# Modulation products spread over the projection and attention preparation, no barriers between layers, DeltaNet blocks read by a gather

## The reference

```python
def modulation(cond, w_mod, b_mod):
    m = jnp.einsum('...d,de->...e', jax.nn.silu(cond), w_mod) + b_mod
    return split_cols(m, (D_MODEL, D_MODEL, D_MODEL))
...
for l in range(DEPTH):
    shift, scale, gate = modulation(c, w_mod[l], b_mod[l])
    h = rms_norm(xs, norm_w[l]) * (1.0 + scale[:, None, :]) + shift[:, None, :]
    out, _ = mixer(h, lp, (cache_k[:, l], cache_v[:, l], state_gdn[:, l], state_ssm[:, l]))
    xs = xs + gate[:, None, :] * out
y_sample = rms_norm(xs, final_norm_w)
```

## Time and profile before

| | us |
|---|---|
| median of 3 runs | 4798.93 (4793.77 to 4803.2) |
| the profiled execution's own time | 4772.26 |
| its span | 4770.5 |
| PE, PEld busy | 4117.2 (86%), 3850.1 (81%) |
| DVE, ACT, POOL busy | 2153.1 (45%), 1038.3 (22%), 600.1 (13%) |
| mean DMA rate | 104 GB/s |

### The profile page before, as it was taken

The page is one execution under the profiler, slowest core; times in us unless marked ns, Lnnn a source line. Parts: engine busy times, 40 slices in busy tenths (PEclk is TensorE's granted clock), DMA queues, the critical chain, the costliest instruction groups (busy, mean ns, idle before and its releaser), DMA issues.

```text
span 4770.5 us, 64010 instructions
## 1 busy us (share of the span) xinstructions
PE 4117.2 (86%) x24849; PEld 3850.1 (81%) x24849; DVE 2153.1 (45%) x2548; ACT 1038.3 (22%) x1855; POOL 600.1 (13%) x725
## 2 busy tenths in 40 slices
PE   6999999974898968868879999999649989678698
PEld 2999999974887838868849999999648877478688
DVE  3432541116665782245345235311266667723563
ACT  2110111013444510220021012010233454102200
POOL 0010000025100150000000000000350002400000
PEclk7999999987998979989989999999859989789799
DMA  6222222225002442533252222222530034435332
GB/s 225 83 90 81 80 89 94 84 93 192 13 14 77 158 159 95 159 120 115 78 182 91 87 79 85 89 93 75 172 102 14 14 100 158 141 109 164 102 123 92
DMA packets 421562, 497.62 MB, mean 104 GB/s; under 512 B 77602, under 2 KB 357508, under 8 KB 413772
## 3 DMA queue, kind: packets, MB, share of 16 engines
q1 hardware_dynamic: 354840, 384.79, 24.5%
q0 software_dynamic: 33856, 94.70, 5.3%
q10 hardware_dynamic: 32636, 15.04, 1.1%
HBM read 325.08 MB, written 169.37 MB: 104 GB/s over the span
## 4 chain that ended last, share of the span: by engine, by line
PE 71%; DVE 7%; DMA 6%; issue 6%; SPq 3%; DVEq 3%; POOL 2%; ACT 1%; POOLq 1%; ACTq 1%
PE PSUM L680 15%; PE PSUM L682 14%; PE PSUM L681 14%; PE PSUM L1121 5%; PE PSUM L1268 4%; PE PSUM L1142 3%; PE PSUM L1110 2%; PE PSUM L1111 2%; SPq L899 2%; PE PSUM L1371 1%; PE PSUM L1372 1%; PE PSUM L1373 1%; DMA g_XY<-xy_d 1%; PE PSUM L1227 1%; DMA xin<-proj_d 1%
## 5 line engine op out<-in xcount | busy, mean ns | idle before, releaser
L680 PE MATMUL PSUM<-h_hi,w_hi 128*128 128x384 f32 x3456 | 1160.3, 336 | 38.2 <-DVEq L526 30.0
L681 PE MATMUL PSUM<-h_lo,w_hi 128*128 128x384 f32 x3456 | 1158.6, 335 | 0.0
L682 PE MATMUL PSUM<-h_hi,w_lo 128*128 128x384 f32 x3456 | 1158.2, 335 | 0.0
L680 PEld LDWEIGHTS PSUM<-h_hi,w_hi 128*128 128x128 f32 x3456 | 652.1, 189 | 39.3 <-issue 30.2
L681 PEld LDWEIGHTS PSUM<-h_lo,w_hi 128*128 128x128 f32 x3456 | 652.2, 189 | 0.0
L682 PEld LDWEIGHTS PSUM<-h_hi,w_lo 128*128 128x128 f32 x3456 | 651.9, 189 | 0.0
L664 DVE CAST w_hi<-w_raw 128x2048 fp32r<-128x2048 f32 (+1 forms) x104 | 118.9, 1143 | 722.6 <-PE PSUM L682 584.1
...
L680 PE MATMUL PSUM<-b_hi,w_hi 128*128 128x384 f32 x768 | 263.7, 343 | 27.9 <-DVE w_lo L666 10.8
L1121 PE MATMUL PSUM<-v_all,prob_t 128*128 128x64 f32 x2336 | 283.6, 276 | 2.3 <-DVE prob_t L2260 2.2
L1121 PEld LDWEIGHTS PSUM<-v_all,prob_t 128*128 128x128 f32 x2336 | 279.1, 196 | 4.6 <-issue 3.5
L681 PE MATMUL PSUM<-b_lo,w_hi 128*128 128x384 f32 x768 | 261.9, 341 | 0.0
...
## 6 DMA issues: line engine op xcount, KB each, us to landing
...
```

The costliest lines, as they stand in the source:

```text
L680: pe.matmul(dst, wh, x_hi[:, k, lo:hi], start=(k == 0), stop=False)
L681: pe.matmul(dst, wh, x_lo[:, k, lo:hi], start=False, stop=False)
L682: last = pe.matmul(dst, wl, x_hi[:, k, lo:hi], start=False, stop=(k == kt - 1))
```

## The change

- *Norm without a stage of its own.* The squares of x are made block by block as the output projection finishes them, and the sums directly after the last; barriers 0 and 13 and the first one are gone. The final norm takes its factors from the same sums.
- *Modulation by rows.* At the start four pieces of 512 columns (shift and scale) have a buffer each. The gate's four pieces of 256 columns are multiplied after each of the first four runs of the projection (`gate_products`), and shift and scale of the next layer in eight pieces of 256 columns, one behind each tile of attention preparation (`next_load`, `next_columns`). The last layer does that too, on the same weights.
- *First group by k.* The projection's first group is multiplied block by block as h is made (`first_group`), with both accumulators in use at once; DVE splits its weights before it makes h.
- *Loads at the start*: four x buffers instead of two, and the small vector loads issued by POOL ahead of everything, for the second layer during the output projection.
- *DeltaNet preparation*: the block stores of SP and POOL are gone, POOL issues each row load as soon as its buffer is filled, and other fills come later.
- *Blocks by gather*: in attention preparation SP reads the blocks out of `gdn_tile_d` into `u_raw`, in 40 transfers of rows of 128 bytes (`blocks_in`).

```diff
-        def blocks_out(e, t, d):
-            for c in range(4):
-                at = slice(c * SOLVE, (c + 1) * SOLVE)
-                src = g_out[t % 2][at, 6 * d].rearrange("p (h t) -> p h t", t=P)[:, :, at]
-                dst = adiag_d[d, c * 32 + t * 4:c * 32 + t * 4 + 4] if t < NS else adiag_p_d[d].rearrange("(h c) n -> c h n", c=4)[c]
-                e.dma_start(dst.rearrange("h (j i) -> j h i", i=SOLVE), src).then_inc((g_pstored if d else g_stored)[t % 2], 16)
+        def blocks_in(e, c, d):
+            at = slice(c * SOLVE, (c + 1) * SOLVE)
+            for h in range(GH):
+                e.dma_start(u_raw[c * 32 + h:c * 32 + 32:GH, d].rearrange("t (j i) -> t j i", i=SOLVE),
+                            gdn_tile_d[0:NS, at, 6 * d, h * P + c * SOLVE:h * P + c * SOLVE + SOLVE]).then_inc(beta_in, 16)
+            e.dma_start(u_raw[32 * d + c:32 * d + 16:4, 2].rearrange("h (j i) -> h j i", i=SOLVE),
+                        gdn_tile_d[NS, at, 6 * d].rearrange("j (h t) -> h j t", t=P)[:, :, at]).then_inc(beta_in, 16)
...
-                if t >= 2:
-                    sp.wait_ge(tok_turned, t - 1)
+                if t >= 4:
+                    sp.wait_ge(tok_turned, t - 3)
                 src = xsm[t * P:(t + 1) * P] if t < NS else A["x_prompt"].rearrange("b t d -> (b t) d")
-                sp.dma_start(x_tok[t % 2][:], src).then_inc(tok_in[t % 2], 16)
-            sp.drain().then_inc(phase_done, 1)
+                sp.dma_start(x_in[t % 4][:], src).then_inc(x_loaded[t % 4], 16)
+            wm = A["w_mod"][0].rearrange("(k p) n -> p k n", p=P)
+            for g in range(4):
+                sp.dma_start(w_mod[g][:], wm[:, :, g * 2 * GW:(g + 1) * 2 * GW]).then_inc(mod_in[g], 16)
+            sp.dma_start(rope[:], rope_table.rearrange("p (t a d) -> p t a d", t=NT, a=2)).then_inc(cst_in, 16)
+            sp.wait_ge(mod_used, 1)
...
+                def gate_load(r):
+                    if r == 0:
+                        for b in range(2):
+                            sp.wait_ge(x_out[b], l * 64 + 64)
+                            sp.sem_inc(waits_held, 1)
+                        sp.wait_ge(h_made, l * KT + KT)
+                    else:
+                        sp.wait_ge(mod_used, gate_done(l, r - 1))
+                    at = 2 * D_MODEL + r * GW
+                    sp.dma_start(w_gate[:], A["w_mod"][l].rearrange("(k p) n -> p k n", p=P)[:, :, at:at + GW]).then_inc(mod_in[2], 16)
...
+                    if run < 4:
+                        gate_load(run)
...
-                    sp.wait_ge(g_stored[p], (l + 1) * (5 - p) * 5 * 16)
-                    sp.wait_ge(g_pstored[p], (l + 1) * (5 - p) * 4 * 16)
-                for d in range(2):
-                    sp.dma_start(u_raw[:, d], adiag_d[d]).then_inc(beta_in, 16)
-                    sp.dma_start(u_raw[32 * d:32 * d + 16, 2], adiag_p_d[d]).then_inc(beta_in, 16)
...
+                    sp.wait_ge(g_stored[p], (l + 1) * (5 - p) * 16)
+                def next_load(g):
+                    if g >= 2:
+                        sp.wait_ge(mod_used, next_done(l, g - 2))
+                    src = A["w_mod"][NEXT].rearrange("(k p) n -> p k n", p=P)
+                    sp.dma_start(w_next[g % 2][:], src[:, :, g * GW:(g + 1) * GW]).then_inc(mod_in[g % 2], 16)
+                next_load(0)
+                next_load(1)
+                for t in range(2, 10):
+                    if t < NT:
+                        sp.wait_ge(transposed, nth(l, t - 1, 1, 5))
+                        ain_load(t, t % 2)
+                    if t >= 4:
+                        next_load(t - 2)
+                    blocks_in(sp, (t - 2) // 2, t % 2)
...
+            def norm_sums(i):
+                pe.wait_ge(n_add, i * (KT - 1) + KT - 1)
+                for t in range(NT):
+                    last = pe.matmul(bank(6, 1, t), tmp[:, t * P:(t + 1) * P], ones[:, 0:1], start=True, stop=True)
+                last.then_inc(n_mm, 1)
+            def mod_product(dst, w):
+                for k in range(KT):
+                    last = pe.matmul(dst, cond[:, k:16:8], w[:, k], start=(k == 0), stop=(k == KT - 1))
+                last.then_inc(mod_used, 1)
...
+            pe.wait_ge(cond_t, 3)
+            for g in range(4):
+                pe.wait_ge(mod_in[g], 16)
+                if g >= 2:
+                    pe.wait_ge(mod_row, g - 1)
+                mod_product(bank(4 + g % 2)[0:2], w_mod[g])
+                if g == 1:
+                    norm_sums(0)
+            pe.wait_ge(mod_row, 4)
+            mod_columns(mod_rows, 16, 7, 0).then_inc(mod_used, 1)
...
+                def first_group():
+                    pe.wait_ge(w_ready[0], split_count(l, 0) + 2)
+                    pe.wait_ge(acc_free[0], l * NG + 1)
                     for k in range(KT):
...
+                        pe.wait_ge(h_made, l * KT + k + 1)
+                        for b in range(2):
+                            wh = w_hi[0][:, k, b * P:b * P + P]
+                            wl = w_lo[0][:, k, b * P:b * P + P]
+                            for c in range(3):
+                                lo, hi = c * THIRD, (c + 1) * THIRD
+                                dst = bank(3 * b + c, THIRD)
+                                pe.matmul(dst, wh, h_hi[:, k, lo:hi], start=(k == 0), stop=False)
+                                pe.matmul(dst, wh, h_lo[:, k, lo:hi], start=False, stop=False)
+                                last = pe.matmul(dst, wl, h_hi[:, k, lo:hi], start=False, stop=(k == KT - 1))
+                            if k == KT - 1:
+                                last.then_inc(acc_ready[b], 1)
+                def gate_products(run):
+                    if run < 4:
+                        if run:
+                            pe.wait_ge(mod_row, rows_done(l, run - 1))
+                        pe.wait_ge(mod_in[2], 16 + (l * 4 + run + 1) * 16)
+                        mod_product(bank(6, GW)[0:2], w_gate)
+                    elif run == 4:
+                        pe.wait_ge(mod_row, rows_done(l, 3))
+                        pe.sem_inc(waits_held, 1)
+                        mod_columns(gate_rows, 8, 7, 0).then_inc(mod_used, 1)
...
+                    begun = 0
+                    if run == 0:
+                        begun = 2
+                        first_group()
+                        multiply_group(pe, l, 1, 1, 0, KT, h_hi, h_lo)
+                    groups(pe, base + begun, 2 * pairs - begun, lambda n, p, m, j: multiply_group(pe, l, n, p, m, KT, h_hi, h_lo))
                     base += 2 * pairs
+                    gate_products(run)
...
+                def next_columns(g):
+                    pe.wait_ge(mod_row, rows_done(l, 4 + g))
+                    pe.sem_inc(waits_held, 1)
+                    last = mod_columns(next_rows[g % 2], 2, 5, GW + 4 * g)
+                    if g == NS - 1:
+                        last.then_inc(mod_used, 1)
...
+                    if t:
+                        next_columns(t - 1)
+                    if t < NS:
+                        pe.wait_ge(mod_in[t % 2], 16 + (l * 4 + t // 2 + 1) * 16)
+                        mod_product(bank(5, GW)[0:2], w_next[t % 2])
...
-                barrier(pe, l, 13)
+                norm_sums(l + 1)
...
+                    if 2 <= t < NS + 2:
+                        act.wait_ge(mod_used, next_done(l, t - 2))
+                        act.activation(next_rows[t % 2][0:2], bank(5, GW)[0:2], ACT.Copy).then_inc(mod_row, 1)
...
-                barrier(act, l, 13)
...
+                for k in range(KT):
+                    act.wait_ge(x_new, l * KT + k + 1)
+                    if k >= 2:
+                        act.wait_ge(n_add, (l + 1) * (KT - 1) + k - 1)
+                    act.activation(row_bc[:] if k else tmp[:], x_sb[:, k], ACT.Square).then_inc(n_sq, 1)
...
-                pool.memset(beta_p[:], 0.0)
                 pool.tensor_tensor(own[:], ident[:, 0:4], ident[:, 4:8], ALU.add)
                 pool.drain()
-                for n in range(2):
+                def rows_fill(n):
                     pool.tensor_scalar(g_row[n][:].rearrange("p d (h t) -> p d h t", t=P),
                                        own[:].unsqueeze(1).unsqueeze(3).broadcast_to([P, 2, GH, P]), -1.0, None, ALU.mult)
                     pool.tensor_copy(g_col[n][:], again(ones, 2))
-                pool.memset(u_raw[:, 2], 0.0)
-                pool.drain().then_inc(g_clear, 1)
-                pool.sem_inc(g_clear, 1)
-                pool.memset(w_inv[:], 0.0)
-                pool.drain()
-                pool.memset(w_inv[:, :, 0:SOLVE * SOLVE:SOLVE + 1], 1.0)
-                pool.memset(u_sol[:, 2], 0.0)
+                    pool.drain()
 
...
-                def blocks_ready(t):
-                    pool.wait_ge(gp_kk, l * NT + t + 1)
-                    pool.sem_inc(waits_held, 1)
-                    blocks_out(pool, t, 1)
+                rows_fill(0)
                 row_load(0)
+                rows_fill(1)
```

(27 more changed lines are left out.)

260 lines of the change are left out of this document (113 added, 147 removed).

## The result

The changed kernel takes 4752.7 us in the median of 4 runs (4739.8 to 4755.9) against 4800.8 for the kernel before: ratio 0.9897, 95% interval 0.9875 to 0.9919. It is 48 us faster where 83 were forecast, 5 us above the stated range of 4672 to 4748. Its profiled execution took 4755.9 us, with a span of 4754.2.

What follows compares the result with a forecast made beforehand. TensorE was taken to bound the projection, DMA DeltaNet preparation and DVE attention preparation. Terms -47, +3, -67.6, +29, -29, +28 and +0.5 sum to -83: profile 4689, median 4716 us, range 4672 to 4748.

Steps and rivals of the forecast that it cites:

- from the first tile at about 6.6 nine end at 19 us: Start: transposes of the nine x tiles follow each other without waiting for loads, ending at 19 us.
- the term of -47: Start of the program: first projection matmul at 67 +-4 us instead of 114.05, so -47 us.
- Projection, +29 and +3: Projection, both layers: gate products and small transposes add 29 us, waiting for the first accumulator half's evacuation adds 3.
- Between the layers, -67.6: Last output matmul to next projection: first h_lo at 24.5 us instead of a 92.2 us stretch, so -67.6 us.
- DeltaNet preparation, -14.5 a layer: DeltaNet preparation: earlier row loads save 8.3 us a layer and removed block stores 6.2.
- 8.3 were forecast: Ahead of DeltaNet preparation: row loads issued after the first fill let TensorE start at 1040.4 instead of 1048.7.
- the 6.2 for the DMA work: DeltaNet preparation: dropping the 72 block stores saves 6.2 us a layer, bounds 0 and -10.
- rival B: DeltaNet preparation keeps 8.0 us a tile; attention preparation drops to 1.2 GHz in gaps, 10.7 a loop; 4739 us; chance 0.20.
- Attention preparation, +15 a layer before the 1.8 of above: Attention preparation: the added product makes TensorE's loop 9.8 us, +15 a layer, bounds +11 and +51.
- the 1.8 of above: End of DeltaNet preparation: of POOL's removed 8.3 us drain only 1.8 is gained, booked in attention preparation.
- Rival A: Attention preparation: the product fits TensorE's idle 40%, tiles stay at DVE's 6.82 us; -28 more, 4688 us; chance 0.19.
- rival D: Attention preparation at low clock throughout, +51 a layer instead of +15; 4788 us, about no change; chance 0.03.

Runs made afterwards that it cites:

- e2: Changed kernel with the 22 small vector loads issued by ScalarE instead of GpSimd, at the start behind the squares; median 4737.7 us, ratio 0.9895.
- e8: Changed kernel with product first in attention preparation, small loads moved to SyncE's queue, earlier ain loads and 19 idle VectorE increments; median 4672.1 us, ratio 0.9747.
- e3: Changed kernel with the small vector loads later on GpSimd's queue: behind the ninth turned x tile, and the output projection's first block; median 4751.1 us, ratio 0.9911.
- e10: Changed kernel without the ten broadcast loads of query and key gains for the second layer; one execution, 4742.1 us.
- e5: Changed kernel with 19 idle semaphore increments in VectorE's program behind the projection; one profiled execution, 4733.3 us.
- e11: The kernel of e5 timed in rounds against the kernel before; median 4738.9 us, ratio 0.988.
- e9: The kernel before with 45 idle semaphore increments in VectorE's program behind the projection; one execution, 4784.4 us.

## Why the prediction was wrong

Three steps of the prediction failed, in this order of size. The small loads for the next layer, which the change moved, had no term: they cost 20 us, 10 a layer. The start's step "from the first tile at about 6.6 nine end at 19 us" left them out too: the tiles ended at 36.5, and the term of -47 came out 15 us too small. And VectorE's moved code had no term: 10 us in the state-space scan. Each stage is held against the executions of the table:

- *Start, -47 forecast.* Measured -29 (about 115 to 85.9); over all profiles -32 (114.1 to 118.7 in three of the kernel before, 81.5 to 85.9 in seven with this start). The transposes of x were to follow each other without waiting for loads; they waited 3.7 us for the fifth tile and 10.8 for the sixth, since GpSimd's loads, now issued ahead of everything, lay beside them. With these moved (e2, e8) the first matmul comes at 73.3 and 73.0, so they are 10 to 12 of the missing 15 us. The rest is `w_mod`, landed at 25.5 in e2 and not 22.5, and products that took 16.6 and 15.2 us there instead of 15.9 and 14.0.
- *Projection, +29 and +3.* Measured +15.5 and +16.2: right.
- *Between the layers, -67.6.* Measured -68.4: right. The norm's power and VectorE's jump back run at the same time, and the jump ends later, by 1.1 us where the forecast had 2.1: GpSimd's `pow` ends at 2399.74, the jump at 2400.88 (chain after).

```profile
2397.66 0.06 DVE stat L2016
2397.74 0.07 DVEq L2030
2397.82 3.06 issue
2401.01 0.35 DVE r_diag L2027 x2
```

- *DeltaNet preparation, -14.5 a layer.* Ahead of it -7.3, where 8.3 were forecast (the prediction's own numbers add up to 1040.9 and 7.8). Of the 6.2 for the DMA work, 4.3 came: VectorE's last block is ready 70.5 us into the stage instead of 74.8, on average over the profiles of either kernel and of the variants that leave this stage alone. SyncE's tile stores are 7.5 us apart in layer 0, between the forecast's 7.2 and the 8.0 of before, so rival B was half right here. From that block to the third turn of `ain` it is 15.2 instead of 19.0, so 3.8 less where the forecast had 1.8. The sum of the two, 8.1 for 8.0, is right by two errors that cancel. As forecast, the removed drain does not count in full: TensorE's wait at the barrier falls from 15.1 to 5.3 us, and its next wait, for the third load of `ain`, grows from 5.4 to 11.3. The table cuts between these two, so it shows -13 in this stage and +17 to +18 in the next.
- *Attention preparation, +15 a layer before the 1.8 of above.* From the third turn of `ain` to the first score it is 78.7 us instead of 67.2: +11.5. The period was 10.16 us for the 9.8 forecast, but only four turns were that far apart, and the end, from the last turn to the first score, took 24.5 us instead of 27.9. Rival A (turns 6.8 apart) and rival D are out. The clock came out between the forecast and rival B: the granted clock was 0.54 (so mostly 1.2 GHz) in the 2.53 us of work behind the wait, and 1.00 over whole periods of e8, which has no such wait. The twelve turns of a tile's heads took 2.53 us where e8 has 1.49, and the product 4.00 where it has 3.62. That is 1.4 us a period, where I had taken 1.0 and rival B 1.9. The Trainium skill's "TensorE: Matmul & The Clock Gate", section "HAM oscillation — how this bites in real kernels", describes bursts between waits that each start cold; the trace agrees, with a granted clock of 0.53 and 0.54 behind two such waits.
- *The two preparations with the step ahead of them* came out at -3.3 us a layer, against about -0.5 in the sum. This helped by 6 in all.
- *What had no term.* The next layer's loads I took for free in the output projection, and didn't look where GpSimd's program really issues them: it passes the two arrivals without waiting for the other engines, so the loads start at 2158.5, right behind barrier 10 and beside the branch weights: +10 us a layer (e3, e10). And the scan lost 5 us a layer by the moved code of VectorE (e5, e11).

The terms: 83, less 15 (start), 20 (branches) and 10 (scan), plus 8 (6 in the preparations, 1 each between the layers and at the end) make 46, and 48 were measured. That it fits so well is in part luck. The profiled executions don't close on it: the kernel before took 4772 and 4798 us, and 4784 in e9, which adds only 45 idle increments, the changed one 4756, so 29 less than their mean. Most of the other 19 us lie in attention, the products of the state space and the DeltaNet scan, which the change doesn't touch and which differ by as much between executions of one program. A difference between two single profiles (16 or 42 us here, by which one of before is taken) could not have told a gain of 48 from one of 20; only the stages could.
